# Seven instead of six extra places for expert weights, with moved norm rows, split conversions and a skipped addition

## The reference

```python
def layer_norm(x, g, b):
    mu = jnp.mean(xf, axis=-1, keepdims=True)
    var = jnp.mean(jnp.square(xf - mu), axis=-1, keepdims=True)
    return ((xf - mu) * lax.rsqrt(var + LN_EPS) * g + b).astype(x.dtype)
...
    def block(xt):
        probs = jax.nn.softmax((xt @ router_w).astype(jnp.float32), axis=-1)
        ...
        h = (jax.nn.silu(jnp.einsum('td,edf->tef', xt, w_gate))
             * jnp.einsum('td,edf->tef', xt, w_up))
        h = h * comb[:, :, None].astype(h.dtype)
        return jnp.einsum('tef,efd->td', h, w_down)
...
    for l in range(DEPTH):
        ...
        x = layer_norm(DEEPNORM_ALPHA * x + mix, ln1_g[l], ln1_b[l])
        ffn = moe_ffn(x, router_w, router_b, moe_w_gate[l], moe_w_up[l], moe_w_down[l])
        x = layer_norm(DEEPNORM_ALPHA * x + ffn, ln2_g[l], ln2_b[l])
```

## Time and profile before

| | us |
|---|---|
| median of 3 runs | 769.87 (769.69 to 771.09) |
| profiled execution | 769.16 |
| its span, first to last instruction | 767.3 |
| TensorE busy | 743.0 |
| VectorE busy | 296.0 |
| ScalarE busy | 241.7 |
| GpSimd busy | 105.4 |
| read from HBM | 244.58 MB |

### The profile page before, as it was taken

The page is one execution under the profiler, slowest core; times in us unless marked ns, Lnnn a source line. Parts: engine busy times, 40 slices in busy tenths (PEclk is TensorE's granted clock), DMA queues, the critical chain, the costliest instruction groups (busy, mean ns, idle before and its releaser), DMA issues.

```text
span 767.3 us, 10640 instructions
## 1 busy us (share of the span) xinstructions
PE 743.0 (97%) x4092; PEld 440.9 (57%) x4093; DVE 296.0 (39%) x537; ACT 241.7 (32%) x454; POOL 105.4 (14%) x68
## 2 busy tenths in 40 slices
PE   9999999999999899999999999999999999999993
PEld 6989887645353353353799888645353454335332
DVE  5589927642111111120667656742111111112115
ACT  5556366242111111120735666332111111112112
POOL 2013000067000000002041000066000000000022
PEclk9999999999999999999999999999999999999997
DMA  9998333889999999999995433789999999995311
GB/s 327 297 390 308 118 110 131 290 354 423 419 422 422 422 422 421 422 422 415 387 389 209 136 139 137 286 361 423 420 422 422 421 422 422 421 422 202 146 55 55
DMA packets 51430, 246.13 MB, mean 321 GB/s; under 512 B 6249, under 2 KB 6466, under 8 KB 26818
## 3 DMA queue, kind: packets, MB, share of 16 engines
q1 hardware_dynamic: 50818, 243.55, 79.9%
q10 hardware_dynamic: 576, 2.10, 1.0%
HBM read 244.58 MB, written 1.05 MB: 320 GB/s over the span
## 4 chain that ended last, share of the span: by engine, by line
PE 82%; DMA 13%; DVE 3%; ACT 1%; issue 1%; SPq 0%; DVEq 0%; ACTq 0%
PE ps L1905 22%; PE ps L1705 14%; PE ps L1917 13%; DMA ring<-in_moe_w_down 12%; PE ps L1700 12%; PE ps L1872 3%; PE ps L1891 3%; PE ps L1956 2%; PE ps L1667 1%; PE ps L1880 1%; PE ps L1988 1%; DMA ring<-in_a_w_in 1%; PE ps L1640 1%; PE ps L1742 1%; PE ps L1661 1%; PE ps L2038 1%
## 5 line engine op out<-in xcount | busy, mean ns | idle before, releaser
L1905 PE MATMUL ps<-ring,scratch 128*64 128x512 f32 x640 | 140.3, 592 | 0.1
L1917 PE MATMUL ps<-ring,scratch 128*64 128x512 f32 x512 | 114.5, 596 | 8.2 <-DMA ring<-in_moe_w_down 8.2
L1905 PEld LDWEIGHTS ps<-ring,scratch 128*64 128x64 f32 x640 | 48.3, 137 | 88.3 <-issue 88.0
L1096 DVE TENSOR_TENSOR ring_lo<-ring,w_hi 128x2048 fp32r<-128x2048 f32 x36 | 83.4, 2331 | 18.3 <-ACT w_hi L728 17.1
L677 POOL TENSOR_TENSOR scratch<-rounded,gate 128x256 f32<-128x256 f32 x16 | 14.1, 884 | 492.8 <-PE ps L2046 309.0
L1917 PEld LDWEIGHTS ps<-ring,scratch 128*64 128x64 f32 x512 | 36.7, 137 | 74.6 <-issue 72.1
L728 ACT ACTIVATE w_hi<-ring 128x2048 fp32r<-128x2048 f32 x35 | 66.7, 1913 | 27.9 <-PE ps L1705 15.7
L1508 DVE TENSOR_TENSOR scratch<-ps,scratch 128x512 f32<-128x512 f32 x16 | 11.1, 692 | 157.1 <-PE ps L1905 157.0
L1519 DVE SCALAR_TENSOR_TENSOR rounded<-ps,gslot,rounded 128x512 fp32r<-128x512 f32 x32 | 24.0, 751 | 106.1 <-ACT rounded L972 106.1
L1905 PE MATMUL ps<-spare,scratch 128*64 128x512 f32 x256 | 56.3, 592 | 0.0
L972 ACT ACTIVATE rounded<-ps,gslot 128x512 fp32r<-128x512 f32 x32 | 22.0, 688 | 99.0 <-PE ps L1917 99.0
(11 more groups left out here) (299 smaller groups left out, 1069.0 us busy)
## 6 DMA issues: line engine op xcount, KB each, us to landing
ring<-in_moe_w_down SPq DMA_DIRECT2D x64, 1024.0 KB, 15.0
ring<-in_moe_w_up SPq DMA_DIRECT2D x48, 1024.0 KB, 14.6
ring<-in_moe_w_gate SPq DMA_DIRECT2D x32, 1024.0 KB, 12.2
spare<-in_moe_w_gate SPq DMA_DIRECT2D x32, 1024.0 KB, 14.9
ring<-in_a_w_in SPq DMA_DIRECT2D x16, 1024.0 KB, 13.2
scratch<-in_moe_w_up SPq DMA_DIRECT2D x16, 1024.0 KB, 19.7
ring<-in_kv_w SPq DMA_DIRECT2D x8, 1024.0 KB, 14.7
ring<-in_a_w_out SPq DMA_DIRECT2D x4, 1024.0 KB, 14.2
```

The costliest lines, as they stand in the source:

```text
L1096: V.tensor_tensor(ring_lo[:, piece_slot(i), :, :], ring[:, piece_slot(i), :, :], w_hi[:, i % HI, :, :].bitcast(F32), ALU.subtract).then_in ...
L1905: last = mm(ps[half, bank, :], xe[:, HALF_K * part + k, own], weight(odd, matrix, part, e)[:, k, :], start=part == 0 and k == 0, stop=part ...
L1917: last = mm(ps[half, bank, :], hT[:, 2 * part + k, half], weight(odd, DOWN, part, e)[:, 2 * k + cols, :], start=part == 0 and k == 0, stop ...
```

## The change

It joins several edits.

- `TWICE` is 7: up's second part for the first expert gets a third place in `late`. The three are at 8 K, at 54 K, and at 0, where `xn` lies. For this the overflow's buffers move over `hid` and `hT`, and the norm rows `ln1_gb` over `ys_hi` and `ys_lo`; ScalarE's first write of `ys_hi` now waits for `affine`.
- Pair 1's extra chunks are loaded in between pair 0's, as their places come free; the norm rows are loaded by SyncE behind them, and no longer by ScalarE.
- The first piece is loaded and converted in two halves of two row blocks each.
- Pair 0 doesn't add up (`pe.If(two > 0)`), and its zero fills go.
- `rstd` has three steps; a memset in `layer_norm` goes; the norm between the layers is written, turned and taken by column halves, with other banks and fewer matmuls on zeros; `normalise_for_experts` works in four halves, the first ahead of the router's exponential; the last norm begins its centring ahead of the root.

The core of the diff:

```diff
-TWICE = 6
+TWICE = 7
...
-TURN_BANKS = (0, 1, BANK_C, BANK_D)
+TURN_BANKS = (BANK_C, BANK_D, 0, 1)
...
-        both_late = at(0, 2, HALF_K, COLS)
-        late = [both_late[:, e, :, :] for e in range(2)]
+        late = [at(first, HALF_K, COLS) for first in (8 * K, 54 * K, 0)]
...
+                if i == 0:
+                    sp.dma_start(ring[:, 0, 0:2, :], w[:, 0:2, :]).then_inc(w_first_in, 16)
+                    sp.dma_start(ring[:, 0, 2:4, :], w[:, 2:4, :]).then_inc(arrive[0], 16)
+                    return
...
-                for matrix, part in order:
-                    if (matrix, part) in FIRST:
-                        load_part(layer, p + 1, 1 - odd, matrix, part, p)
+                for matrix, part, es in order:
+                    if chunk_of(matrix, part, es[0]) < TWICE:
+                        load_part(layer, p + 1, 1 - odd, matrix, part, es, p)
...
-            FIRST = ((GATE, 0), (GATE, 1), (UP, 0))
-            REST = ((UP, 1), (DOWN, 0), (DOWN, 1))
+            FIRST = ((GATE, 0, BOTH), (GATE, 1, BOTH), (UP, 0, BOTH), (UP, 1, (0,)))
+            REST = ((UP, 1, (1,)), (DOWN, 0, BOTH), (DOWN, 1, BOTH))
...
-                for part in range(2):
-                    for e in range(2):
-                        load_chunk(layer, 1, 1, GATE, part, e)
-                if layer:
-                    sp.wait_ge(x_affine, 2)
-                load_chunk(layer, 1, 1, UP, 0, 1)
+                    if c == 7:
+                        load_chunk(layer, 1, 1, GATE, 1, 1)
+                    if c == 8:
+                        if layer:
+                            sp.wait_ge(x_affine, 2)
+                        load_chunk(layer, 1, 1, UP, 0, 0)
+                    if c > 8:
+                        load_chunk(layer, 1, 1, GATE, *divmod((last - RING + c) % HI, 2))
+                    if c == 10:
+                        load_chunk(layer, 1, 1, UP, 0, 1)
+                for j, name in enumerate(("ln1_g", "ln1_b")):
+                    row = ins[name][layer:layer + 1, :]
+                    sp.dma_start(ln1_gb[:, j, :], row.broadcast_to([P, D])).then_inc(ln_in, 16)
                 sp.wait_ge(xe_ps, GATHERS * layer + 1)
                 sp.wait_ge(xr_ready, 2 * layer + 2)
-                load_chunk(layer, 1, 1, UP, 0, 0)
+                load_chunk(layer, 1, 1, UP, 1, 0)
...
-                    nc.scalar.activation(w_hi[:, 0, :, 0:T], ring[:, 0, :, 0:T], ACT.Copy).then_inc(w_first, 1)
-                    nc.scalar.activation(w_hi[:, 0, :, T:2 * T], ring[:, 0, :, T:2 * T], ACT.Copy).then_inc(hi_ready, 1)
+                    nc.scalar.activation(w_hi[:, 0, 2:4, :], ring[:, 0, 2:4, :], ACT.Copy).then_inc(hi_ready, 1)
...
             input_high(0)
+            act.wait_ge(w_first_in, 16)
+            nc.scalar.activation(w_hi[:, 0, 0:2, :], ring[:, 0, 0:2, :], ACT.Copy).then_inc(w_first, 1)
             high(0)
...
-                step(V.tensor_tensor(t, first, first, ALU.mult))
+                step(V.scalar_tensor_tensor(t, first, -0.5, first, ALU.mult, ALU.mult))
                 step(V.tensor_tensor(t, t, var, ALU.mult))
-                step(V.tensor_scalar(t, t, -0.5, 1.5, ALU.mult, ALU.add))
-                return V.tensor_tensor(y, first, t, ALU.mult)
+                return V.scalar_tensor_tensor(y, t, 1.5, first, ALU.add, ALU.mult)
...
-                    V.tensor_scalar(x[:, 0, :], ps[:, 0:2, :].rearrange("p b n -> p (b n)"), mv[:, 0, 0:1],
-                                    rs[:, 2, 0:1], ALU.subtract, ALU.mult).then_inc(x_done[0], 1)
+                    for half in range(2):
+                        V.tensor_scalar(x[:, 0, half * COLS:(half + 1) * COLS], ps[:, half, :], mv[:, 0, 0:1],
+                                        rs[:, 2, 0:1], ALU.subtract, ALU.mult).then_inc(x_half[0], 1)
...
-                for t in range(TT):
-                    pe.wait_ge(x_done[t], 2)
-                    for k in range(KT):
-                        last = turn(x, t, k, TURN_BANKS[k // 2])
+                for half in range(2):
+                    for t in range(TT):
+                        pe.wait_ge(x_half[t], half + 1)
+                        for k in range(HALF_K * half, HALF_K * (half + 1)):
+                            last = turn(x, t, k, TURN_BANKS[k // 2])
...
-                    if not odd:
-                        add_up(0)
-                    add_up(1).then_inc(acc_ps, 1)
+                    if odd:
+                        add_up(1)
+                    else:
+                        with pe.If(two > 0):
+                            add_up(0)
+                            add_up(1)
```

More of the change, by code:

```diff
@@ L294, in build @@
         x_done = [sem(f"x_done{t}") for t in range(TT)]
+        x_half = [sem(f"x_half{t}") for t in range(TT)]
         xn_step = sem("xn_step")
@@ L520, in _, with load_part @@
                     load_router()
-            def load_part(layer, index, odd, matrix, part, pairs):
+            def load_part(layer, index, odd, matrix, part, es, pairs):
                 sp.wait_ge(*chunk_read(PAIRS * layer + pairs, matrix, part))
@@ L709, in _ @@
         def _(act):
-            def load_ln(i):
-                layer, which = divmod(i, 2)
-                assert which == 0
-                for j, name in enumerate(("ln1_g", "ln1_b")):
-                    row = ins[name][layer:layer + 1, :]
-                    act.dma_start(ln1_gb[:, j, :], row.broadcast_to([P, D])).then_inc(ln_in, 16)
             act.wait_ge(consts_ready, 1)
@@ L937, in moe @@
                 act.wait_ge(router_in, ROUTER)
-                act.wait_ge(routed, layer + 1)
-                for half in range(2):
-                    nc.scalar.activation(ys_hi[:, half * COLS:(half + 1) * COLS], seg[:, :], ACT.Copy, scale=0.0
-                                         ).then_inc(ys_act, 1)
+                act.sem_inc(ys_act, 2)
                 take_xe(xc_ps, layer + 1, BANK_C, range(0, 4), columns_of(0))
-                act.wait_ge(x_done[0], 2 * layer + 1)
-                act.wait_ge(x_done[1], 2 * layer + 1)
+                act.wait_ge(x_done[0], 2 * layer + 2)
+                act.wait_ge(x_done[1], 2 * layer + 2)
                 nc.scalar.activation(xr_hi.rearrange("p t n -> p (t n)"), xn.rearrange("p t n -> p (t n)"),
@@ L1077, in _ @@
             second_parts(1)
+            normalise_for_experts(2, 0, 0)
             router_exp(1)
-            normalise_for_experts(2)
+            normalise_for_experts(2, 0, 1)
+            for half in range(2):
+                normalise_for_experts(2, 1, half)
             moe(1)
@@ L1425, in route @@
                 pick_slots(0, 2, 2)
-                for half in range(2):
-                    V.tensor_scalar(ys_lo[:, half * COLS:(half + 1) * COLS], seg[:, :], 0.0, None, ALU.mult
-                                    ).then_inc(ys_dve, 1)
-                V.tensor_scalar(put[:, :], seg[:, 0:T], 0.0, None, ALU.mult).then_inc(put_done, 1)
+                dve.sem_inc(ys_dve, 2)
+                dve.sem_inc(put_done, 1)
                 step(V.reciprocal(rg[:, 1, 0:TT], m2))
@@ L1643, in turn_normed @@
             def turn_normed():
-                for t in range(TT):
-                    pe.wait_ge(x_done[t], 2)
-                    for k in range(KT):
-                        last = turn(x, t, k, TURN_BANKS[k // 2])
-                        if t == 1 and k % 2:
-                            last.then_inc(tp_ready, 1)
+                for half in range(2):
+                    for t in range(TT):
+                        pe.wait_ge(x_half[t], half + 1)
+                        for k in range(HALF_K * half, HALF_K * (half + 1)):
+                            last = turn(x, t, k, TURN_BANKS[k // 2])
+                            if t == 1 and k % 2:
+                                last.then_inc(tp_ready, 1)
             def turn_half(half, value):
@@ L1688, in piece @@
                         pe.wait_ge(lo_ready, i + 1)
[L1689 to L1691 removed]
+                    if i == number == 0:
+                        for ks in (range(2), range(2, HALF_K)):
+                            if ks.start:
+                                pe.wait_ge(hi_ready, 1)
+                            for j, c, k in itertools.product(range(2), range(2), ks):
+                                mm(ps[:, 4 + j, c * T:(c + 1) * T], w[:, k, (2 * j + c) * P:(2 * j + c + 1) * P], xs[:, k, :],
+                                   start=c == 0 and k == 0, stop=k == HALF_K - 1, skip_group_check=True)
+                    for j in range(0 if i == number == 0 else 2):
                         bank = 4 + 2 * (n % 2) + j
@@ L1728, in _ @@
             nothing_long(BANK_D)
-            for _ in range(2):
-                nothing(BANK_D)
+            nothing(BANK_D)
             def scores(hp):
@@ L2077, in _ @@
             moe(0)
-            for _ in range(2):
-                nothing(BANK_A)
-            for _ in range(40):
+            for _ in range(36):
                 nothing(BANK_A, COLS // 2)
```

(4 more changed lines are left out.)

90 lines of the change are left out of this document (51 added, 39 removed).

## The result

The changed kernel takes 766.43 us (median of 5 runs, 765.58 to 766.96), beside 770.29 for the kernel before (5 runs, 769.69 to 771.09): ratio 0.9949, 95% interval 0.9935 to 0.9964. The profiled execution has 764.4 us of span instead of 767.3, 2.9 less. Measured a second time the two stood at 767.11 and 770.16, ratio 0.9963 (0.9949 to 0.9977). The forecast was 767.1, 2.8 less than the 769.87 it started from; by the medians the gain was 3.9 us the first time and 3.1 the second.

The account below looks back on a forecast made before the run. Bound: in each layer the DMA stream until pair 4's last down half lands, then 78.4 us of TensorE; outside the MoE, engine hand-overs. 0.57 + 1.4 + 0.2 + 0.5 + 0.1 = 2.8 us off 769.87 gives 767.1, range 765.7 to 769.0.

Parts of the forecast that it names:

- The third place and the new order: MoE weight loads: pair 3's last down chunk stays the 36th after the stream's restart, so 0 us in both layers.
- rival 1: MoE loads: the third place does lift the waits, giving 755 us, or 762 with the naive 2.5 per layer; chance 0.07.
- The skipped addition: Pair 0 of each layer: 1.85 us saved by removing eight matmuls becomes waiting before pair 3's first down half; worth 0.
- the sign that the prediction named for it: TensorE's waits for down weights sum to about 12 us instead of 8.2, some 2.5 before pair 3's first down half.
- First piece: Kernel start: loading and converting the first piece in halves starts TensorE's projection at 8.80 instead of 9.40; 0.57 us, bounds 0 and 0.62.
- Between the layers: Norm between the layers by halves, fewer fillers, one root step fewer: 1.4 us, bounds 0.8 and 1.6.
- Both limits that the step named: Between the layers: TensorE's projection could start at 377.6; VectorE's chain to the low part of the weights ends at 381.7.
- Second attention half: Before the second attention half, the root's one step fewer is on the chain: 0.2 us, bounds 0 and 0.2.
- MoE starts: Start of each MoE, zero fills gone and normalising split: 0.05 us per layer, 0.1 in all, bounds 0 and 0.3.
- MoE lengths: First expert matmul to residual matmuls: gain 0 in both layers, the distance staying 208.3 us in layer 0.
- Last norm: Kernel end: a shorter root and earlier first centring let VectorE's last row end sooner; 0.5 us, bounds 0.2 and 0.75.
- The slower rival: MoE: a 2.5 us idle hole before pair 3's down half lowers TensorE's clock, giving 771 us; chance 0.05.

Follow-up runs that it names:

- experiment 1: The changed kernel with only six of the next pair's gate and up halves ahead of a pair's down weights (TWICE = 6): 762.07 us.
- experiment 8: The kernel of experiment 1 with its second early up chunk asked for behind the wait for `xn`'s place instead of ahead of it: 766.61 us.
- Experiment 4: The changed kernel with 16 matmuls on zeros put into each layer's first pair, where the eight adding ones are skipped: 766.32 us.
- Experiment 6: The kernel before, with GpSimd's last two operations cut from 512 columns to 1: VectorE's rows take 1.28 and 0.75 us instead of 2.07 and 0.98.
- Experiment 2: The changed kernel with a pair's down weights asked for ahead of the next pair's gate and up halves from pair 4 on: 763.23 us.
- experiment 7: The changed kernel with the halves between the layers undone (whole tiles): residual matmuls to projection 11.3 us, 10.4 with halves; span 764.2 us.
- experiment 9: The changed kernel with six early halves and down weights first from pair 4, minus one 512-column f32 matmul on zeros at the start: 760.17 us, beside 759.77.

## Why the prediction was right

By its own steps:

- **The third place and the new order, 0.** Right, and for the reason given. Pair 3's last down chunk lands where it did (259.04, 258.98), and experiments 1 and 8 show that one chunk across the restart decides: 762.1 against 766.6. A place that isn't tied to `xn` was worth 3.5 us by the layers' lengths and 4.4 by the medians; the longer list of early halves that came with it took them back. The lower of rival 1's two gains (762) is what was there to be had, without this list.
- **The skipped addition, 0.** Right in sum, wrong in its account, and the sign that the prediction named for it didn't come: the waits for down weights are 9.4 us, not about 12. The step said that 1.85 us would be saved in pair 0 and the wait before pair 3's first down half would grow to 2.5. Pair 0 got 0.49 shorter (27.35 to 26.86 us), since the eight matmuls had covered TensorE's wait for ScalarE's copy, and that wait became 1.31, with 0.42 more at pair 2's up weights. The prediction looked for what hides the saving behind it and not for what the removed work itself had hidden. Experiment 4 shows that work added to pair 0 is taken up by the waits. The branch itself is misread in the prediction: the matmuls are skipped in pair 0 alone, not in pair 6, where the eight take 1.85 us as before.
- **First piece, 0.57.** It measured 0.77. The halves took the piece out of the chain, as the step said, but the size is another's: the chain of the start is now TensorE's own matmuls, and executions with this start differ by 1.3 us in it (7.64 to 8.91). The bounds of 0 to 0.62 missed that; that the profiled execution came near 0.57 is in part luck.
- **Between the layers, 1.4.** 1.26 (0.45 to 1.71). Both limits that the step named are there, the projection 1.5 us sooner and the low part 1.26.
- **Second attention half, 0.2.** 0.15.
- **MoE starts, 0.1.** 0 in both (0.77 to 0.73, 1.86 to 1.85).
- **MoE lengths, 0.** 0.28 and 0.06 longer. Layer 0's 0.28 is a balance. The landing at 288.86 stood still while TensorE entered 0.73 sooner, so up to it the layer is 0.78 longer; behind it it is 0.50 shorter (77.94 instead of 78.44), all in pair 7 (23.99 to 23.48), whose loads the prediction had as coming in time already and that part as fixed.
- **Last norm, 0.5.** 1.1, beyond the bound of 0.75. The step took each row's time as fixed and looked no further than VectorE's last row. VectorE's part from the residual matmuls to its end is 1.50 us shorter (12.48 to 10.98): 0.2 from the root and the memset, 0.5 from the half row moved ahead, 0.79 because the row of 1024 columns no longer waits for GpSimd. Experiment 6 shows that this was a wait. But GpSimd is last now, and from the residual matmuls to its end it is 12.10, so only 0.38 of the 1.50 counts. The other 0.7 us lie behind the last operation (3.2 to 2.4 us): before, both last stores were issued after it, now one of them is issued while GpSimd still works. How much of the 0.7 that makes, no run shows.
- **The slower rival.** It didn't come: in 195 to 262 us, with 3.0 us of idle TensorE, the granted clock reads 1.00. Its hole of 2.5 us didn't come either, the longest is 1.32. Experiment 2 has one of 2.35 us (at 248.71), and there the granted clock reads 1.00 in 246 to 249 and in 249 to 252, and the matmuls behind it take 0.59 us each as elsewhere.

```profile
195.00:262.00 67.00, 63.95 (x314) 1.00 1.01 422
```

With the leads' differences added (0.77 - 0.04 - 0.28 + 1.26 + 0.15 - 0.01 - 0.06 + 1.1) it is 2.9 us: two terms too small by 0.8 together, the others too large by 0.7. That these cancel is luck.

## What to carry to other kernels

Where a stream of loads is the bound, count the transfers between the moment it restarts and the one that is waited for; an extra buffer gains only if it takes a transfer out of that count, at most by that transfer's time, and a prefetch list made longer by it puts the transfer back. Read for each stage which landing is the last that is waited for (here pair 3's and 4's down weights, then pair 7's up weights), and order the loads by these. Before a piece of work is removed, ask also what it covers: the wait behind it may be nearly as long.

## What the hardware showed that I had not expected

**VectorE and GpSimd.** The eight durations at the two ends (four before, four after, of rows with both inputs in SBUF) fit one rule to about 0.1 us: an operation of VectorE with two inputs in SBUF and one of GpSimd, which here reads SBUF too, exclude each other, the first to start goes through, and the other shows its wait inside its own duration. After: GpSimd's 2.15 (758.14) is a wait until 759.16, when VectorE's 1.28 ends, and 1.13 of its own; VectorE's 0.97 (759.87) a wait for GpSimd's end at 760.29 and 0.55; GpSimd's 1.59 a wait until 760.84 and 1.12. VectorE's 0.74 at 759.09, with one input in PSUM, ran through beside GpSimd. The Trainium skill (SBUF — State Buffer, SBUF: two separate sides) has this rule, with the lock held for the whole instruction; the trace agrees.

**TensorE's start.** Two f32 matmuls on zeros take 1.97 us at 3.48 and 1.07 at 7.15 of the changed kernel. The ratio, 1.84, is near that of the clock's two levels (2.4 and 1.2 GHz), while the windows' granted clock reads 1.00 in both; that it is the clock isn't shown:

```profile
3.00:4.00 1.00, 1.00 (x3) 0.33 (x3) 0.00 (x0) 0.00 (x0) 0.74 (x5) 1.00 0.78 254
...
7.00:8.00 1.00, 1.00 (x5) 0.19 (x2) 0.69 (x1) 0.96 (x2) 0.00 (x0) 1.00 1.03 336
```

The moment of the change differs between executions with the same instructions at the start: the first projection stood at 7.64 in experiment 7 and at 8.63 in the changed kernel. With one filler fewer (experiment 9) it stood at 9.27.
